# A transformer layer with 32 experts: experts put in order of load on chip, the 14 lightest computed as raw fp32 products on two 64-column tiles

## The reference

```python
logits = h @ router_w + router_b                 # 512 tokens, 32 experts
top_vals, top_idx = lax.top_k(logits, 4); gates = softmax(top_vals)
gu = xb @ w_gu[e] + b_gu[e]                      # [1024] -> [2048]
gate, up = split(gu); gate = min(gate, 7); up = clip(up, -7, 7)
y = ((up + 1) * gate * sigmoid(1.702 * gate)) @ w_down[e] + b_down[e]
out = x + g2 * sum over the 4 experts of a token (gate * y); then a final norm
```

## Time and profile before

| what | us |
|---|---|
| median of 3 runs (lowest, highest) | 1501.27 (1499.06, 1501.77) |
| span of the profiled execution, first to last instruction | 1494.1 |
| the median less that span | 7.2 |
| first bias matmul of item 0 | 347.61 |
| first bias matmul of item 31 | 1429.78 |
| rows of item 31 scaled (L2106 starts) | 1475.33 |

### The profile page before, as it was taken

How to read it: one execution, slowest core, us unless ns; L and a number is a source line. 1 busy time by engine, 2 the same in 40 slices (tenths; PEclk the granted TensorE clock), 3 DMA queues, 4 the chain that set the end, 5 groups by cost and what they waited for, 6 DMA issues and landing times.

```text
span 1494.1 us, 21340 instructions
## 1 busy us (share of the span) xinstructions
PE 1459.7 (98%) x7139; PEld 1149.1 (77%) x7139; DVE 1257.1 (84%) x1146; ACT 1062.7 (71%) x1122; POOL 375.6 (25%) x267
## 2 busy tenths in 40 slices
PE   4999999999999999999999999999999999999997
PEld 1667974567888888888888888888888888888885
DVE  0576765358999999999999999999999999999997
ACT  3542334546887888788888888888788888888883
POOL 1000020203122233322223333222223332222251
PEclk9999999999999999999999999999999999999999
DMA  9655620066899999999999999999999999999994
GB/s 347 214 160 203 223 103 15 27 233 250 344 375 369 375 368 373 370 368 373 371 377 383 370 383 376 372 364 371 374 369 379 373 370 369 377 372 372 384 369 151
DMA packets 95076, 474.96 MB, mean 318 GB/s; under 512 B 23748, under 2 KB 33964, under 8 KB 42816
## 3 DMA queue, kind: packets, MB, share of 16 engines
q1 hardware_dynamic: 82656, 451.39, 78.0%
q0 software_dynamic: 12304, 22.97, 5.5%
q10 hardware_dynamic: 80, 0.13, 0.0%
HBM read 468.16 MB, written 23.09 MB: 329 GB/s over the span
## 4 chain that ended last, share of the span: by engine, by line
PE 92%; DMA 3%; ACT 2%; DVE 1%; issue 0%; SPq 0%; DVEq 0%; ACTq 0%
PE bank L1587 16%; PE bank L1590 15%; PE bank L1594 15%; PE bank L1615 7%; PE bank L1623 7%; PE bank L1616 7%; PE bank L1389 4%; PE bank L1201 3%; PE bank L1203 3%; PE bank L1202 3%; DMA area<-bias_g_parts 2%; PE bank L1563 2%; PE bank L1555 2%; PE bank L1156 1%; PE bank L1362 1%; PE bank L1579 1%
## 5 line engine op out<-in xcount | busy, mean ns | idle before, releaser
L1812 DVE TENSOR_TENSOR e_lo<-ring,e_hi 128x2048 fp32r<-128x2048 f32 x384 | 865.7, 2288 | 62.2 <-ACT e_hi L808 61.3
L808 ACT ACTIVATE e_hi<-ring 128x2048 fp32r<-128x2048 f32 x384 | 728.1, 1920 | 208.3 <-PE bank L1594 207.1
L1587 PE MATMUL bank<-e_hi,x_hi 128*128 128x512 f32 x1024 | 403.7, 394 | 0.0
L1590 PE MATMUL bank<-e_hi,x_lo 128*128 128x512 f32 x1024 | 399.5, 390 | 0.0
L1594 PE MATMUL bank<-e_lo,x_hi 128*128 128x512 f32 x1024 | 274.1, 390 | 0.0
L1587 PEld LDWEIGHTS bank<-e_hi,x_hi 128*128 128x128 f32 x1024 | 192.3, 188 | 46.5 <-issue 7.2
L1594 PEld LDWEIGHTS bank<-e_lo,x_hi 128*128 128x128 f32 x1024 | 192.4, 188 | 40.3
L1590 PEld LDWEIGHTS bank<-e_hi,x_lo 128*128 128x128 f32 x1024 | 192.5, 188 | 39.0
L1615 PE MATMUL bank<-e_hi,act_hi 128*128 128x512 f32 x496 | 196.3, 396 | 0.0
L1616 PE MATMUL bank<-e_hi,act_lo 128*128 128x512 f32 x496 | 193.5, 390 | 0.0
L741 POOL COPY future<-routes 128x1 int32 (+1 forms) x31 | 81.6, 2631 | 366.8 <-DVE area L2116 366.8
(11 more groups left out here) (270 smaller groups left out, 1575.1 us busy)
## 6 DMA issues: line engine op xcount, KB each, us to landing
ring<-in_w_gu SPq DMA_DIRECT2D x256, 1024.0 KB, 9.0
ring<-in_w_down SPq DMA_DIRECT2D x128, 1024.0 KB, 7.2
ring<-in_ada_w SPq DMA_DIRECT2D x24, 1024.0 KB, 9.1
ring<-in_w_in SPq DMA_DIRECT2D x9, 1024.0 KB, 7.9
ring<-in_w_o SPq DMA_DIRECT2D x4, 1024.0 KB, 5.8
xs<-in_x SPq DMA_DIRECT2D x4, 512.0 KB, 4.7
ring<-in_w_in SPq DMA_DIRECT2D x8, 256.0 KB, 5.6
xn_rows<-area POOLq DMA_DIRECT2D x4, 512.0 KB, 5.0
```

What stands on the lines that cost most here:

```text
L808: return nc.scalar.activation(dst, src, ACT.Copy, scale=scale)
L1587: pe.matmul(bank[b][:], x_hi[:, c, :], hi, start=False, stop=False)
L1590: pe.matmul(bank[b][:], x_lo[:, c, :], hi, start=False, stop=False)
L1812: tt(e_lo[c % PARTS][:], raw(period.raw_slot(c)), e_hi[:, c % PARTS, :].bitcast(F32), ALU.subtract).then_inc(lo_ready, 1)
```

## The change

Routing also counts each expert's tokens and ranks the experts. Items 0 and 1 stay experts 0 and 1, items 2 to 17 are the next in order of load, items 18 to 31 are the 14 lightest. SP reads each item's expert number from a small table before it loads its weights. The lists of rows are put into the same order, and a light item keeps 64 slots (its tokens beyond 64, none here, would go to the branch).

A light item isn't split: PE takes the raw chunk as fp32 and 64 columns of tokens as the stationary operand. Of the output, alternate 512-column blocks go to partitions 0 to 63 and 64 to 127 of a bank, so that neighbouring matmuls are on different halves of the array: 4 matmuls of 64x512 to a chunk in place of 12 of 128x512. ACT and DVE do none of the chunk work then, a slot is free when PE has used it (`chunk_used`), and the second half of the down rows is moved to partitions 0 to 63 by ACT. The small loads of the biases stay behind chunk 4. All 32 periods are written out; the hardware loops are gone. `done(...)` waits for the instruction in it.

```diff
+ORDER = "HH" + "H" * 16 + "L" * 14
+NARROW = 64
+assert len(ORDER) == E and ORDER[:2] == "HH" and ORDER[-1] == "L"
+N_WIDE = ORDER.count("H")
...
+N_NARROW = E - N_WIDE
...
+LOAD_RANK = [ORDER[:p].count("H") if m == "H" else N_WIDE + ORDER[:p].count("L") for p, m in enumerate(ORDER)]
...
             def raw_free(period, c):
 
-                sp.wait_ge(lo_ready, period.at(c) - (SLOTS - 1))
-
-
-
-            def up_bias(e):
-
+                before = period.at(c) - SLOTS
+                if isinstance(before, int) and before < MAIN_CHUNKS and not chunk_wide(before):
+                    sp.wait_ge(chunk_used, before + 1)
+                else:
+                    sp.wait_ge(lo_ready, splits_before(before) + 1)
+
+
+
+            def up_bias(i, e):
+
+                if i is not 0:
+                    sp.wait_ge(bias_used, i)
...
-            def steady(i, e, e_before):
+            def gate_up_chunks(i, e):
                 period = Later(i)
                 for c in range(GU):
                     raw_free(period, c)
                     gu_chunk(period, c, e)
                     if c == 4:
-                        up_bias(e)
+                        up_bias(i, e)
+
+            def down_chunks(i, e_before):
+                period = Later(i)
                 for q in range(DN):
                     raw_free(period, GU + q)
                     down_chunk(period, GU + q, q, e_before)
...
             opening(0, 0)
-            with sp.Fori(1, E) as i:
-                steady(i, i, i - 1)
-            closing(E, E - 1)
-            sp.wait_ge(lo_ready, Later(E).at(0))
+            e_before, e = 0, 1
+            for i in range(1, E):
+                gate_up_chunks(i, e)
+                if i == 1:
+                    sp.wait_ge(tables_ready, 1)
+                if i + 1 < E:
+                    e_next = sp.value_load(expert_at[0:1, i + 1:i + 2], min_val=0, max_val=E - 1)
+                down_chunks(i, e_before)
+                e_before, e = e, e_next
+            closing(E, e_before)
+            raw_free(Later(E), DN)
...
             def opening(i):
+                if i == 0:
+                    pool.wait_ge(tables_ready, 1)
                 bring(i, slice(i + 2, i + 3))
...
-                    a.wait_ge(chunk_used, period.at(c) - (PARTS - 1))
+                if not isinstance(n, int) or n >= MAIN_CHUNKS:
+                    a.wait_ge(chunk_used, n - (PARTS - 1))
+                elif splits_before(n) >= PARTS:
+                    a.wait_ge(chunk_used, SPLIT_CHUNKS[splits_before(n) - PARTS] + 1)
                 copy(e_hi[:, c % PARTS, :], raw(period.raw_slot(c))).then_inc(hi_ready, 1)
...
+            def mixed(i):
+
                 period, after = Later(i), Later(i + 1)
                 act_parts(i)
+                if wide(i):
+                    for c in range(PARTS, GU):
+                        hi(period, c)
+                early = GU if not wide(i - 1) else CHUNKS if wide(i) else GU + 2
+                for c in range(GU, early):
                     hi(period, c)
                 glu(i, period.at(GU))
+                if i + 1 < E:
+                    x_parts(i + 1)
+                if wide(i - 1):
+                    for c in range(early, CHUNKS):
+                        hi(period, c)
+                if i + 1 < E and wide(i + 1):
+                    for c in range(PARTS):
+                        hi(after, c)
+                if i + 1 == E:
+                    for half in range(2):
+                        a.wait_ge(at_full, 2 * E + (half - 1))
+                        copy(last_actT[:, 2 * half:2 * half + 2, :],
+                             bank[6 + half][:, 0:256].rearrange("p (k n) -> p k n", k=2)).then_inc(ahi_ready, 1)
+                upper_rows(i)
...
 
                 pe.wait_ge(table_in, 3)
+                pe.matmul(bank[4][:, 64:64 + E], tab[0:E, :], chosen[0:E, :], start=True, stop=True)
+                pe.matmul(bank[4][0:1, 96:96 + E], eid[0:E, :], chosen[0:E, :], start=True, stop=True)
...
+            def gate_up_narrow(period):
+
+                i = period.i
+                pe.wait_ge(g_rows_in, i * 64 + 64)
+                pe.wait_ge(xt_taken, i * 2 + 2)
+                pe.wait_ge(up_ready, i)
+                pe.wait_ge(glu_ready, i)
+                for g in range(4):
+                    rows, half = slice(32 * g, 32 * g + 3), slice(NARROW * (g % 2), NARROW * (g % 2) + NARROW)
+                    mm = pe.matmul(bank[g // 2][half, :], ones_b[rows, 0:NARROW], bias_g[rows, :], start=True,
+                                   stop=False)
+                mm.then_inc(bias_used, 1)
+                for c in range(GU):
+                    pe.wait_ge(*period.landed(c))
+                    w = raw(period.raw_slot(c))
+                    for g in range(4):
+                        half = slice(NARROW * (g % 2), NARROW * (g % 2) + NARROW)
+                        mm = pe.matmul(bank[g // 2][half, :], xgT[:, c, 0:NARROW], w[:, 512 * g:512 * g + 512],
+                                       start=False, stop=(c == GU - 1))
+                    mm.then_inc(chunk_used, 1)
+
+            def down_narrow(period, c0, out, turned, between=None):
+
+                i = period.i
+                pe.wait_ge(y_ready, i)
+                pe.wait_ge(ahi_ready, i * 2)
+                for n in range(DN):
+                    pe.wait_ge(*period.landed(c0 + n))
+                    w = raw(period.raw_slot(c0 + n))
+                    for k in range(2):
+                        left = turned[:, 2 * (n % 2) + k, NARROW * (n // 2):NARROW * (n // 2) + NARROW]
+                        for q in range(2):
+                            mm = pe.matmul(out[NARROW * q:NARROW * q + NARROW, :], left,
+                                           w[:, k * D + q * 512:k * D + q * 512 + 512],
+                                           start=(n == 0 and k == 0), stop=(n == DN - 1 and k == 1))
+                    mm.then_inc(chunk_used, 1)
+                    if between is not None and n == 2:
+                        between()
...
+            def order_experts():
+
+                e = slice(0, E)
+                v.wait_ge(order_consts, 1)
+                done(stt(out=load[e, :], in0=dbank(D_["c3"])[e, E:2 * E], scalar=float(E), in1=tie[e, :], op0=ALU.mult,
+                         op1=ALU.add))
+                done(tt(ahead[e, :], load[e, :], ident[e, 0:E], ALU.mult))
+                done(nc.vector.tensor_reduce(my_load[e, :], ahead[e, :], AX.X, ALU.add))
+                done(ts(ahead[e, :], load[e, :], my_load[e, :], None, ALU.is_gt))
+                done(nc.vector.tensor_reduce(my_rank[e, :], ahead[e, :], AX.X, ALU.add))
+                done(ts(chosen[e, :], load_rank[e, :], my_rank[e, :], None, ALU.is_equal))
+                done(ts(is_narrow[e, :], my_rank[e, :], float(N_WIDE), None, ALU.is_ge))
+
+            order_experts()
...
-            done(nc.vector.tensor_copy(dstf[:, 0:E], tabT[:, 0:E]))
-            lists(0, E).then_inc(lists_ready, 1)
+            done(nc.vector.tensor_copy(dstf[:, 0:2], tabT[:, 0:2]))
+            lists(0, 2).then_inc(lists_ready, 1)
             lo(Opening(0), 4)
             lo(Opening(0), 5)
             v.wait_ge(table_full, 1)
             done(nc.vector.tensor_copy(tab, bank[5][:, 0:P]))
+            done(ts(beyond[E:2 * E, :], tab[0:E, NARROW:P], is_narrow[0:E, :], None, ALU.mult))
+            done(tt(tab[E:2 * E, NARROW:P], tab[E:2 * E, NARROW:P], beyond[E:2 * E, :], ALU.add))
...
+            done(nc.vector.tensor_copy(expert_at[:], bank[4][0:1, 96:96 + E]))
+            done(tt(dstf[:, 2:E], bank[4][:, 66:64 + E], keep_rows[:, 2:E], ALU.mult))
+            lists(2, 48).then_inc(tables_ready, 1)
...
+            def narrow_rows(rows, sums, moved, scale, count):
+
+                n = slice(0, NARROW)
+                stt(out=rows[n, 0:512], in0=sums[n, :], scalar=scale[n, :], in1=g2_row[n, 0:512], op0=ALU.mult,
+                    op1=ALU.mult)
+                v.wait_ge(upper_moved, count)
+                stt(out=rows[n, 512:1024], in0=moved[n, :], scalar=scale[n, :], in1=g2_row[n, 512:1024], op0=ALU.mult,
+                    op1=ALU.mult).then_inc(y_ready, 1)
 
```

More of the change, by code:

```diff
@@ L1015, in x_parts @@
                     last.then_inc(xt_taken, 1)
+                    if isinstance(i, int) and not wide(i):
+                        continue
                     a.wait_ge(xt_taken, i * 2 + (half + 1))
@@ L1022, in act_parts @@
                     a.wait_ge(at_full, i * 2 + (half - 1))
+                    if isinstance(i, int) and not wide(i - 1):
+                        copy(actT[:, 2 * half:2 * half + 2, :],
+                             bank[6 + half][:, 0:256].rearrange("p (k n) -> p k n", k=2)).then_inc(ahi_ready, 1)
+                        continue
                     copy(act_hi[:, 4 * half:4 * half + 4, :],
@@ L1027, in glu, with upper_rows @@
                 a.wait_ge(chunk_used, full)
```

(43 more changed lines are left out.)

180 lines of the change are left out of this document (101 added, 79 removed).

## The result

The changed kernel takes 1529.05 us (median of 4 runs, 1526.42 to 1535.69) against 1500.98 for the kernel before on the same chip: ratio 1.0205, interval 1.0178 to 1.0232. It is slower, as forecast, and inside the range; but the forecast was +8 us and the measurement is +28. The span of its profiled execution is 1525.9, 31.8 more than before. The spans differ by more than the medians because of the kernel before: in every run for which both are recorded, the time is 1.7 to 1.9 us more than the span, so its profiled execution took about 1496 us (an estimate, 1494.1 + 1.8), some 5 us less than its median. Of the 7.2 us that stand "around" that span above, only 1.8 lie around it; the forecast of 1509 doesn't change by that, since it was added to the median.

What follows compares the result with a forecast made beforehand. PE was taken to bound the kernel at 35.11 us an item, with DMA close behind. Light periods +17, the end -11 and routing +2 gave +8 on 1501.3, so 1509 us, range 1480 to 1545.

Steps and rivals of the forecast that it cites:

- wide items cost the same: Wide items keep 144 split matmuls and 35.11 us each; writing out the loops was priced at 0.
- The light periods: Items 18 to 31: 13 periods of 36.4 us in place of 35.11, +17 us, from -9 to +60.
- 0.3 to the first product, 1.8 for chunk 0, 0.1 for SP: Light period, from the bias matmul until SP issues chunk 6, part of 7.8 us between the landings of chunks 4 and 6.
- PE cold each period: Rival: PE's clock at half when it resumes in each light period, P = 39, 1543 us; chance 0.08.
- the forecast's own hole: Light period, behind chunk 5: PE waits for the biases, so chunk 6 lands 7.8 us after chunk 4, not 5.0.
- gathers and adds: With gate rows, their share of the DMA engines in a light period: 5.2 us at most, 1.5 falling behind chunk 5.
- The end: Item 31, from its bias to scaling its rows: 34.3 us where it was 45.5; -11 us (-13 to -8).
- Routing: Ordering the experts, small DVE operations of 2.0 us before item 1, delays PE nearly whole: +2 us (0 to +3).
- The hole closes: Rival: add and gather land behind chunk 5 of light periods, loads otherwise back to back, P = 34.4, 1483 us; chance 0.30.
- The instruction stream: Rival: written-out code's instruction fetches load a DMA engine, wide periods grow by up to 1.0 us, 1534 us; chance 0.17.
- No overlap of the halves: Rival: a light chunk's two 64-column halves don't overlap, 3.4 us a chunk, 43.5 an item, 1612 us; chance 0.05.
- A drain between products and transposes: Light items on PE: changing the tiling mode drains the engine; unpriced, would lengthen the item's 24 us but stay below the loads.

Runs made afterwards that it cites:

- experiment 1: Also written bias_first: biases issued ahead of chunk 0 instead of behind chunk 4, against the changed kernel; 1476.48 us, ratio 0.9845 to the kernel before.
- experiment 3: Changed kernel plus 36 or 52 extra unread PE products while PE would wait for light items' biases; 1524.02 us with 36, 1515.81 us with 52.
- gates_early: Changed kernel with GpSimd gathering an item's gate rows ahead of the next item's row gather instead of behind it; 1542.63 us, ratio 1.0298.

## Why the prediction was right in sign and short in size

**What held.** PE falls out of the bound; wide items cost the same; in each light period PE stands and is released by the bias DMA, for 9.5 us or more in all but the first (5.7); chunk 6 of items 19 to 31 lands 4.7 to 5.1 after its issue in all but one; a light chunk's products take 1.94 (I took 1.8). Slower was the right side for the right reason: moving the biases turns +28 us into -22.

**The light periods: +17 forecast, +32 measured.** The term that was too small is "0.3 to the first product, 1.8 for chunk 0, 0.1 for SP", 2.2 in all, which measured 4.4, because chunk 0 is computed at half clock. I did see that the clock could fall, but used it only for the upper bound and gave "PE cold each period" 0.08 as a rival of its own. In fact it is a consequence of the forecast's own hole and belonged into the forecast. By this term above all, the time from the landing of chunk 4 to that of chunk 6 is 10.2 on average, 8.2 to 11.7, in the twelve periods to items 20 to 31, against 7.8 (each worked out from issues and landings, as above for item 22). One more term was off, the other way: gathers and adds take 3.8 a period (experiment 1), not 5.2. How much of it falls into the hole no run measured; the sum meets the measured period with 1.3, as 10.2 + 24.9 + 3.8 - 1.3 = 37.6, where I had 1.5. So the error of the hole (+2.4) and that of the traffic (-1.4 + 0.2) partly cancelled. That the period with the clock kept up is 36.3, next to my 36.4, is luck in part for the same reason.

**The end: -11 forecast, -6.7 measured.** Chunk 6 of item 31 lands 9.4 after the bias matmul, not 7.0, for the same reason. And the last chunk is computed at half clock again, after a wait of 1.9 us for it. PE's timeline, the last two chunks of the kernel after:

```profile
1499.54 1.94 PE L1759 MATMUL bank<-ring,last_actT 128*64 128x512 f32 x8 [0.54 <-DMA ring<-in_w_down]
...
1503.62 3.60 PE L1759 MATMUL bank<-ring,last_actT 128*64 128x512 f32 x8 [1.89 <-DMA ring<-in_w_down]
```

**Routing: +2 forecast, +5.9 measured.** From item 0 to item 1 the changed kernels take 28.1 to 29.0 us against 26.85. `order_experts` is there, seven operations of DVE from 358.76 to 360.27, and was priced about right. The other 3.7 lie ahead of item 0, whose bias matmul comes at 351.32 here against 347.61 before, and I priced nothing there. The last of the router's products starts at 337.74 before and at 338.91 after: 1.2 us of the 3.7 are there already, and are scatter between executions, since these starts lie between 337.3 and 339.2 in all traces. From there to the bias matmul, the windows of the kernels before, after and bias_first:

```profile
337.74:347.61 9.87, 8.92 (x66) 6.92 (x66) 6.12 (x14) 6.86 (x13) 2.87 (x4) 1.00 0.63 227
```

```profile
338.91:351.32 12.41, 11.40 (x73) 9.45 (x74) 6.11 (x14) 6.87 (x13) 2.87 (x4) 0.86 0.55 181
```

```profile
338.61:349.88 11.27, 10.05 (x73) 7.88 (x73) 6.09 (x14) 6.86 (x13) 2.87 (x4) 1.00 0.55 199
```

At full clock the changed kernel's way there is about 1.4 us longer, nearly all of it the added products that count the tokens (L1566, 1.05 us and a wait of 0.26 ahead of them in bias_first; 11.27 - 9.87 = 1.4, and the three other changed kernels whose clock stays up there show 11.3 too). The changed kernel's clock is at half for a part of that stretch, 0.86 on average, which makes another 1.1. It isn't so in each execution: item 0 starts between 348.7 and 354.1 in the changed kernels, whose code up to there is the same.

**The rivals.** *The hole closes* was refuted for this kernel and came true with the biases first, at 33.73, under its own 34.4. The HBM limit of about 358 GB/s for a core that the Trainium skill, "DMA: Bandwidth & Descriptors", Specifications, gives, as half of what two cores share, does not show here, where one core runs the kernel: 387 GB/s over 270 us in bias_first. *PE cold each period* is what happened, with 37.6 us a period in place of its 39. *The instruction stream*: q8 brought 53 packets in place of 22, q14 36 in place of 14, and wide periods stayed at 35.11; the rule of the Trainium skill, "Runtime: NRT & Kernel Launch", Instruction fetch mechanics, that such fetches are mostly hidden, is borne out. *No overlap of the halves*: 8 records of a chunk in 1.94 us is two rounds at 0.97, where four whole products of 0.81 would be 3.2, so they overlap. A drain between products and transposes, which the prediction left without a price, shows in no idle time: around 1205.17 in bias_first the last chunk's products, four transposes and the next bias matmul follow each other without a pause.

## What to carry to other kernels

When work is taken off the busiest engine, look for the small transfer that its slowness had hidden: here 12 KB of biases behind the fifth of six loads, harmless while PE was the bound, kept the 12 MB of each light item waiting. Put what starts a stage ahead of the loads that only feed it, or at least so early that the loads issued behind it last longer than wait, first step and one load's latency (here 7.3 to 9.2 us, from 2.5 or 4.4 to the release of chunk 0 and 4.8 for the load). And when the forecast has an engine stand still, price what comes behind it with the clock that the engine will have then.

## What the runs showed of the hardware that I had not expected

- PE stopped for 5.5 us after 8 us of filler work and was at half clock when it resumed (experiment 3); at the end 1.9 us of waiting, after a stretch in which PE was busy 1.94 us of every 2.5, came before a chunk that took 3.60. In bias_first, with pauses of 0.5 to 2.1 us throughout, the mean clock stayed at 0.98 all the same.
- A gather of the gate rows, 4 bytes a token, takes 7.3 to 8.4 us from issue to the release of DVE in the light periods, while weight loads fill the queues: for instance issued at 1152.99, DVE released at 1160.78. DVE waited for it in 12 of the light periods, up to 10.4 us, and taking that wait away made the kernel slower.
- The DMA engines held 387 GB/s at a busy share of 0.99 for 270 us beside gathers and adds; 421 in the cleanest stretch.
- Left open: why periods of 36.4 and 39 alternate in the changed kernel. In the long ones the biases' matmul started 0.9 to 2.4 us behind chunk 4, in the short ones at most 0.8; the add was issued 8.6 us ahead of it in the long period before item 22 and 5.3 in the short one after it. In gates_early, where the add is issued 9.5 to 12.3 us ahead of the biases' matmul from item 20 on, every one of these periods takes 38 us or more. That fits the add as what makes a period long; why early and late adds take turns in the changed kernel, no run tells.
